# Query/key head norms of a fused decoder step: GpSimd's two multiplies go to VectorE, which reads the projections from PSUM

## The reference

```python
proj = rms_norm(x, norm_mix_g) @ w_in_ab      # 1024 -> 2*512 (GLU) + 512 q + 512 k + 512 v + 8 gates
q = rms_norm(q.reshape(*lead, H_B, HEAD_DIM), q_g)     # 8 heads of 64, one gain vector of 64
k = rms_norm(k.reshape(*lead, H_B, HEAD_DIM), k_g)     # k is also an output
glu = val * sigmoid(gate)                     # causal depthwise convolution of 31 taps, LayerNorm, swish
s = q @ k.T * HEAD_DIM ** -0.5 + F_q - F_k    # F: cumulative log forget gates; then softmax, @ v
```

## Time and profile before

| | us |
|---|---|
| median of 3 runs (lowest, highest) | 1314.85 (1314.0, 1315.89) |
| the profiled execution, its own time | 1313.07 |
| its span | 1311.3 |
| PE busy, share of the span | 1252.4, 96% |
| DVE busy | 625.4, 48% |
| ACT busy | 458.4, 35% |
| POOL busy | 165.7, 13% |
| the 30 steps of queries, keys and values | 83.2 to 204.9 |

### The profile page before, as it was taken

How to read it: one execution, slowest core, us unless ns; L and a number is a source line. 1 busy time by engine, 2 the same in 40 slices (tenths; PEclk the granted TensorE clock), 3 DMA queues, 4 the chain that set the end, 5 groups by cost and what they waited for, 6 DMA issues and landing times.

```text
span 1311.3 us, 22853 instructions
## 1 busy us (share of the span) xinstructions
PE 1252.4 (96%) x9658; PEld 1198.9 (91%) x9658; DVE 625.4 (48%) x860; ACT 458.4 (35%) x725; POOL 165.7 (13%) x181
## 2 busy tenths in 40 slices
PE   6987898889999999999999999989999999999998
PEld 5977885456999999999999999989999999999998
DVE  5597698745353343334244344664533342433431
ACT  5624435544343132132133334533421321321321
POOL 3036740100210000000000222042000000000000
PEclk9998998989999999999999999999999999999999
DMA  5321231133232322322222221213223223222211
GB/s 153 100 79 36 82 124 41 49 129 97 85 109 97 97 67 96 96 88 72 96 97 79 84 97 65 97 37 97 67 95 97 91 71 97 96 72 88 97 65 68
DMA packets 111755, 113.17 MB, mean 86 GB/s; under 512 B 6414, under 2 KB 105882, under 8 KB 111663
## 3 DMA queue, kind: packets, MB, share of 16 engines
q1 hardware_dynamic: 110111, 107.50, 25.4%
q0 software_dynamic: 1472, 4.44, 1.1%
q10 hardware_dynamic: 88, 0.02, 0.0%
HBM read 107.21 MB, written 5.16 MB: 86 GB/s over the span
## 4 chain that ended last, share of the span: by engine, by line
PE 82%; DVE 8%; POOL 4%; ACT 2%; issue 2%; DMA 1%; SPq 0%; ACTq 0%; POOLq 0%; DVEq 0%
PE ps L668 75%; DVE c_f L1521 3%; PE ps L859 2%; POOL nat_buf L571 2%; POOL nat_buf L578 1%; DMA w_raw<-in_w_in_ab 1%; PE ps L837 1%; PE ps L814 1%; DVE w_lo L1445 1%; PE ps L850 1%; DVE prob L1618 1%; POOL A_lo L643 1%; DVE a_f L1836 1%; ACT nat_sq L1189 1%; POOL nat_buf L576 0%
## 5 line engine op out<-in xcount | busy, mean ns | idle before, releaser
L668 PE MATMUL ps<-A_hi,w_hi 128*128 128x272 f32 x1408 | 293.2, 289 | 8.1 <-DVE xT L1471 4.0
L668 PE MATMUL ps<-A_lo,w_hi 128*128 128x272 f32 x1408 | 291.8, 289 | 0.0
L668 PE MATMUL ps<-A_hi,w_lo 128*128 128x272 f32 x1408 | 290.8, 288 | 0.0
L1110 ACT ACTIVATE w_hi<-w_raw 128x1024 fp32r<-128x1024 f32 x180 | 189.0, 1050 | 266.0 <-DVE xT L1733 249.2
L668 PE MATMUL ps<-B_hi,w_hi 128*128 128x272 f32 x1280 | 265.9, 289 | 0.0
L668 PE MATMUL ps<-B_lo,w_hi 128*128 128x272 f32 x1280 | 265.0, 288 | 0.0
L668 PE MATMUL ps<-B_hi,w_lo 128*128 128x272 f32 x1280 | 263.9, 288 | 0.0
L668 PEld LDWEIGHTS ps<-A_hi,w_hi 128*128 128x128 f32 x1408 | 221.7, 189 | 9.7 <-ACT xT L1140 4.4
L1445 DVE TENSOR_TENSOR w_lo<-w_raw,w_hi 128x1024 fp32r<-128x1024 f32 x180 | 220.3, 1224 | 4.7 <-ACT w_hi L1110 4.7
L668 PEld LDWEIGHTS ps<-A_hi,w_lo 128*128 128x128 f32 x1408 | 221.7, 189 | 0.0
L668 PEld LDWEIGHTS ps<-A_lo,w_hi 128*128 128x128 f32 x1408 | 220.4, 189 | 0.0
(11 more groups left out here) (273 smaller groups left out, 1057.0 us busy)
## 6 DMA issues: line engine op xcount, KB each, us to landing
w_raw<-in_w_ff_up SPq DMA_DIRECT2D x64, 512.0 KB, 4.4
w_raw<-in_w_ff_down SPq DMA_DIRECT2D x64, 512.0 KB, 4.3
w_raw<-in_w_in_ab SPq DMA_DIRECT2D x20, 512.0 KB, 4.7
w_raw<-in_w_in_c SPq DMA_DIRECT2D x16, 512.0 KB, 3.9
w_raw<-in_w_out_ab SPq DMA_DIRECT2D x8, 512.0 KB, 4.5
k_pg<-in_cache_k SPq DMA_DIRECT2D x16, 256.0 KB, 4.1
v_pg<-in_cache_v SPq DMA_DIRECT2D x16, 256.0 KB, 3.2
w_raw<-in_w_out_c SPq DMA_DIRECT2D x8, 512.0 KB, 4.0
```

Of the source, the lines that this page charges most:

```text
L668: mm = pe.matmul(ps[:, 2 * s + half, 0:HALF], wt[:, j % 4, k, :], mv[:, k, half * HALF:(half + 1) * HALF], start=(k == 0 and at_ == 0), st ...
L1110: act.activation(w_hi[:, j % 4], w_raw[:, b % 2, :, P * (j % 2):P * (j % 2) + P], ACT.Copy)\
```

## The change

POOL's two multiplies and ACT's copy `nat_raw` go away. DVE now does per step: the sums, then for the step before it the reciprocal, a multiply of the reciprocals by `r_nat` (128x4), a multiply of the PSUM bank by them into `nat_buf`, and for keys alone a multiply by the key gain. The query gain (times 1/8) is applied by ACT's copy of the transposed heads, as a scale per partition (`q_gain`, 66x1, with ones for the two forget rows). POOL copies the forget columns and stores keys. The square of step m no longer waits for POOL, but for the sums of step m - 2 (`nat_rs`). PE waits for DVE's product (`nat_evac`, `nat_ready`) and for POOL's columns (`cols_ok`). `nat_evac` is raised by DVE for steps 0 to 19, `v_evac` by ACT for the value steps. The convolution is dealt out anew: 19 in the GLU part (the last GLU step has 2 in place of 5), 3 in each query step, 2 in each key step, the value steps as before, and 19 in attention (where 16 were left before). `split_lo(11, 11)` moves from ahead of step 0 into step 1.

```diff
-CONV_GLU, CONV_QK, CONV_V = [6, 6, 5, 5], (2, 3), 4
-CONV_ATT = [1] * 18 + [0] * 14
+CONV_GLU, CONV_Q, CONV_K, CONV_V = [6, 6, 5, 2], (3, 3), (2, 2), 4
+CONV_ATT = [1] * 19 + [0] * 13
...
+            link(pool.memset(q_gain[:, :], 1.0))
+            pool.dma_start(q_gain[0:HD, :], i["q_norm_g"].rearrange("a d -> d a")).then_inc(q_gain_in, 16)
+            pool.dma_start(k_gain[:, :], i["k_norm_g"][0:1, :].broadcast_to([P, HD])).then_inc(bc_in, 16)
...
+            for m in range(4 * TT):
+                forget_columns(m)
+                if m - 1 >= 2 * TT:
+                    store_keys(m - 1)
...
-                pe.wait_ge(nat_ready, m + 1)
+                if m < 2 * TT:
+                    pe.wait_ge(nat_evac, m + 1)
+                else:
+                    pe.wait_ge(nat_ready, m + 1 - 2 * TT)
+                pe.wait_ge(cols_ok, m + 1)
...
                     if m >= 2:
-                        act.wait_ge(nat_ready, m - 1)
+                        act.wait_ge(nat_rs, m - 1)
                     act.activation(nat_sq[0:n, m % 2, :], src, ACT.Square, scale=r_nat[0:n, t:t + 1]).then_inc(nat_sq_done, 1)
-                    act.activation(nat_raw[0:n, m % 2, :], src, ACT.Copy, scale=r_nat[0:n, t:t + 1]).then_inc(nat_evac, 1)
...
-                               ACT.Copy).then_inc(aug_evac, 1)
+                               ACT.Copy, scale=q_gain[:, :] if m // TT < 2 else 1.0).then_inc(aug_evac, 1)
...
+            def scale_heads(m):
...
+                dve.wait_ge(nat_sqrt, m + 1)
+                link(dve.reciprocal(head, n_small[0:n, 2 + m % 2, :]))
+                link(dve.tensor_scalar(head, head, r_nat[0:n, t:t + 1], None, ALU.mult))
+                if m >= 3:
+                    dve.wait_ge(aug_done, m - 2)
+                    if m - 3 >= 2 * TT:
+                        dve.wait_ge(k_stored[m % 3], 16 * len([u for u in range(2 * TT, m - 2) if u % 3 == m % 3]))
+                dve.tensor_tensor(buf, ps[0:n, m % 4, 0:256].rearrange("p (h d) -> p h d", h=4),
+                                  head.rearrange("p (h a) -> p h a", a=1).broadcast_to([n, 4, HD]), ALU.mult)\
+                   .then_inc(nat_evac, 1)
+                if blk >= 2:
+                    dve.wait_ge(nat_evac, m + 1)
+                    dve.tensor_tensor(buf, buf, k_gain[0:n, :].rearrange("p (a d) -> p a d", a=1).broadcast_to([n, 4, HD]),
+                                      ALU.mult).then_inc(nat_ready, 1)
...
-            split_lo(11, 11)
...
                 if 1 <= m < 4 * TT + 1:
-                    head_factor(m - 1)
+                    scale_heads(m - 1)
+                if m == 1:
+                    split_lo(11, 11)
```

More of the change, by code:

```diff
@@ L159, in build @@
         conv_wT = sb("conv_wT", [P, CT, 32], F32)
-        qk_gain = sb("qk_gain", [P, 2, HD], F32)
+        k_gain = sb("k_gain", [P, HD], F32)
+        q_gain = sb("q_gain", [HD + 2, 1], F32)
         bf_c = sb("bf_c", [H, 1], F32)
@@ L404, in keys @@
                 if b == 0:
-                    sp.wait_ge(nat_ready, 4 * TT)
+                    sp.wait_ge(nat_ready, 2 * TT)
                 if b == 2:
@@ L558, in _, with forget_columns @@
                 pool.tensor_tensor(prod[c % 2][:, :, :, :], window, taps, ALU.mult).then_inc(prod_done, 1)
-            for m in range(4 * TT):
+            def forget_columns(m):
                 blk, t = m // TT, m % TT
                 n = NS if t == 0 else P
-                buf, head = nat_buf[0:n, m % 3], n_small[0:n, 4 + m % 2, :]
-                pool.wait_ge(head_ok, m + 1)
-                pool.wait_ge(nat_evac, m + 1)
+                if m == 0:
+                    pool.wait_ge(fc_ok, 1)
                 if m >= 3:
@@ L570, in _, with store_keys @@
                         pool.wait_ge(k_stored[m % 3], 16 * len([u for u in range(2 * TT, m - 2) if u % 3 == m % 3]))
[L571 to L587, removed]
+                pool.tensor_copy(nat_buf[0:n, m % 3, :, HD:HD + 2],
+                                 f_aug[0:n, blk // 2, H * t + 4 * (blk % 2):H * t + 4 * (blk % 2) + 4, :]).then_inc(cols_ok, 1)
+            def store_keys(m):
+                blk, t = m // TT, m % TT
+                n, h0 = (NS if t == 0 else P), 4 * (blk - 2)
+                pool.wait_ge(nat_ready, m + 1 - 2 * TT)
+                dst = (o["k_sample"][0].rearrange("b q h d -> (b q) h d")[:, h0:h0 + 4, :] if t == 0 else
+                       o["k_prompt"][0, 0, P * (t - 1):P * t, h0:h0 + 4, :])
+                pool.dma_start(dst, nat_buf[0:n, m % 3, :, 0:HD]).then_inc(k_stored[m % 3], 16)
+            for m in range(4 * TT):
+                forget_columns(m)
+                if m - 1 >= 2 * TT:
+                    store_keys(m - 1)
+            store_keys(4 * TT - 1)
+            pool.wait_ge(v_evac, 2 * TT)
             store(o["v_prompt"][0, 0].rearrange("(t p) h d -> p t (h d)", p=P), v_nat[:, 1:TT, :])
@@ L826, in _ @@
                     pe.wait_ge(lo_done, N_NAT + 2 * blk + 2)
-                if m >= 4:
+                if 4 <= m < 4 * TT + 4:
                     pe.wait_ge(nat_evac, m - 3)
+                if m >= 4 * TT + 4:
+                    pe.wait_ge(v_evac, m - 4 * TT - 3)
                 if m == 2:
@@ L1203, in aug_copy @@
                 dst, h0 = (qT if m // TT < 2 else kT), 4 * (m // TT % 2)
+                if m == 0:
+                    act.wait_ge(gain_ok, 1)
                 act.wait_ge(aug_done, m + 1)
@@ L1581, in sums @@
                                   AX_X, ALU.add).then_inc(nat_rs, 1)
-            def head_factor(m):
-                n = NS if m % TT == 0 else P
+            def scale_heads(m):
+                blk, t = m // TT, m % TT
+                n = NS if t == 0 else P
+                head, buf = n_small[0:n, 4 + m % 2, :], nat_buf[0:n, m % 3, :, 0:HD]
                 dve.wait_ge(nat_sqrt, m + 1)
-                if m >= 2:
-                    dve.wait_ge(nat_ready, m - 1)
-                dve.reciprocal(n_small[0:n, 4 + m % 2, :], n_small[0:n, 2 + m % 2, :]).then_inc(head_ok, 1)
-            split_lo(11, 11)
+                link(dve.reciprocal(head, n_small[0:n, 2 + m % 2, :]))
[11 more added lines that the diff above has]
+                                      ALU.mult).then_inc(nat_ready, 1)
             dve.wait_ge(glu_done, CT)
```

17 lines of the change are left out of this document (8 added, 9 removed).

## The result

The changed kernel takes 1298.52 us (median of 4 runs, 1297.32 to 1299.46) against 1314.42 (1310.26 to 1315.89), a ratio of 0.9884 with a 95% interval of 0.9859 to 0.9908. Its profiled execution took 1299.2 us, its span is 1297.5. Measured again on another chip, it took 1301.0 against 1313.14, a ratio of 0.991 (0.9894 to 0.9926). Forecast were 1301.6 and a gain of 13.2; the two measurements gave 15.9 and 12.1, the two profiled spans 13.8.

The account below looks back on a forecast made before the run. The prediction took the ring over ACT, DVE and POOL, 4.4 us a step against PE's 3.46, as the bound. Gain 14.4 less 1.2 in attention made 13.2: 1314.85 - 13.2 = 1301.6 us, range 1297.5 to 1308.

Parts of the forecast that it names:

- The ring: Query, key and value steps: ACT's square, DVE's reciprocal, POOL's two multiplies, next square; 4.4 us per step, gone after the change.
- PE's waits: Before the transposes in query steps: PE waits for DVE's products six times, 0.1 to 1.2 us each, 4.3 in all.
- no stretch below full clock: Sign to look for in the profile after: the granted clock stays full between 91 and 190 us.
- The rival of the clock: PE's query-step gaps keep the clock low; two or three half-clock steps cost 2.1 us each: 1304 to 1306; chance 0.10.
- DVE's list: DVE's work from 90.43 to attention's first maximum: 97.7 us, ending at 188.1 alone, 190.2 with 2.1 of waiting.
- that rival: Convolutions beside POOL's copies and stores keep 0.80 us, not 0.663: 1306 to 1311; chance 0.14, shared with a costlier norm.
- The norm: DVE, each query or key step: reciprocal 0.20, small multiply 0.20, product from PSUM 0.33, together 0.73 us.
- The two first convolutions: DVE, behind `glu_new` at the start of its list: counted at 0.663 us each, like all convolutions.
- PE's list: PE's own work from 91.59: 93.8 us, ending at 185.4 alone; 3.46 us per undisturbed step.
- What attention gives back: Three more convolutions at attention steps 16, 17 and 18 cost 1.2 us, between 0 and 2.0.
- The sum: Whole kernel: gain 14.4 less 1.2 given back in attention, net 13.2 us, for 1301.6 us.
- the stretch: From the GLU transposes to attention step 0's maximum; the maximum moves from 204.57 to 190.2, gaining 14.4 us.

Follow-up runs that it names:

- the first experiments: New convolution tables and `w_lo` place alone on the kernel before: 1313.73 us, ratio 0.9992; conversely, the changed kernel with the old ones: 1303.46 us, ratio 0.9901.
- the deep buffers: Kernel before, POOL's multiplies kept, four buffers instead of two for `nat_raw` and reciprocals, square waiting for sums of m - 2: 1308.83 us, ratio 0.9954.
- the run whose longest wait for a product was 0.8: Changed kernel with ACT's copy first and without the `r_nat` multiply, plus two last-GLU-step convolutions moved to attention: 1301.28 us, ratio 0.9905.
- after: The changed kernel itself, against the kernel before: 1298.52 us, ratio 0.9884; measured again on another chip, 1301.0 us, ratio 0.991.

## Why the prediction was right, step by step

**The ring and its end.** Right: both directions of the first experiments and the waits show it. I had seen only the ring over ACT. The second ring, through the reciprocal that stands behind the next sums on DVE, was in neither the prediction nor my expectation of the deep buffers. The change leaves that order as it was, but takes POOL's multiplies out of the ring. A turn is then some 4.9 us for two steps (matmuls 2.87, square 0.48, sums 0.33, norm 0.81, transposes 0.44; an estimate from rows of this section and of the chains), less than PE's own list. So the number did not suffer, and that was luck and not foresight.

**PE's waits, 4.3 foretold, 5.2 measured.** The size is right, the places are not. I had six waits of at most 1.2, all for DVE. The first is 2.53, which brought back 1.2 GHz for three us ("no stretch below full clock" failed, at a price of 14 matmuls at 0.21 in place of 0.12 from start to start, 1.3 us). The rival of the clock was right that it falls again, for a shorter time than it supposed; in the run whose longest wait for a product was 0.8 it did not fall. Three of 2.1 together are for ACT's copy, which I had costed at nothing. ACT's timeline after:

```profile
112.50 0.30 ACT L1206 ACTIVATE n_small<-n_small,eps 32x4 f32<-32x4 f32 x1 [2.78 <-DVE n_small L1591]
112.70 0.66 ACT L1215 ACTIVATE qT<-ps,q_gain 66x512 f32<-66x512 f32 x1
```

The copy stands behind the root, the root waits for DVE's sums, and PE waited 1.01 us for the copy at 113.51.

**DVE's list, 99.8 foretold (with 2.1 of waits), 101.3 measured** (90.20 to 191.51). DVE's timeline after, beside the earlier trace rows:

```profile
90.20 3.31 DVE L1532 SCALAR_TENSOR_TENSOR c_f<-glu_p,conv_wT,c_f 128x512 f32<-128x512 f32 x2
93.42 0.40 DVE L1591 TENSOR_REDUCE n_small<-nat_sq 32x4 f32<-32x256 f32 x1
93.75 2.06 DVE L1532 SCALAR_TENSOR_TENSOR c_f<-glu_p,conv_wT,c_f 128x512 f32<-128x512 f32 x3
...
104.46 0.41 DVE L1591 TENSOR_REDUCE n_small<-nat_sq 128x4 f32<-128x256 f32 x1
104.79 0.16 DVE L1600 RECIPROCAL n_small<-n_small 128x4 f32<-128x4 f32 x1
104.99 0.23 DVE L1601 TENSOR_SCALAR n_small<-n_small,r_nat 128x4 f32<-128x4 f32 x1
105.25 0.42 DVE L1606 TENSOR_TENSOR nat_buf<-ps,n_small 128x256 f32<-128x256 f32 x1
105.60 2.06 DVE L1532 SCALAR_TENSOR_TENSOR c_f<-glu_p,conv_wT,c_f 128x512 f32<-128x512 f32 x3
...
138.10 0.16 DVE L1600 RECIPROCAL n_small<-n_small 128x4 f32<-128x4 f32 x1
...
139.01 0.43 DVE L1611 TENSOR_TENSOR nat_buf<-nat_buf,k_gain 128x256 f32<-128x256 f32 x1
139.36 1.41 DVE L1532 SCALAR_TENSOR_TENSOR c_f<-glu_p,conv_wT,c_f 128x512 f32<-128x512 f32 x2
...
175.60 15.98 DVE L1532 SCALAR_TENSOR_TENSOR c_f<-glu_p,conv_wT,c_f 128x512 f32<-128x512 f32 x24
191.51 0.28 DVE L1635 TENSOR_REDUCE soft<-ps 128x1 f32<-128x128 f32 x1
```

- The convolution, (191.51 - 175.60) / 24 = 0.663: right, beside POOL's copies too (2.06 for three at 105.60, with a copy from 106.43), so that rival falls.
- Sums 0.33 for 0.34; the product 105.60 - 105.25 = 0.35 for 0.33. The rule of the Trainium skill (VectorE: DVE Perf Modes, The TRN2 errata), 0.39 by estimate, is further off than the row that I took; the busy time of the product was 0.42.
- The norm, 105.60 - 104.79 = 0.81 for 0.73: the term of the sum that was sized too low, by about 1.5 us over 20 (0.08 for each of 16, 0.05 for the four of the sampled tokens). The small multiply took 0.26 to its follower where I had put 0.20, the price of the reciprocal. A key's norm with its gain took 139.36 - 138.10 = 1.26, 0.45 more than a query's, as foretold.
- The two first convolutions took 3.31 where two alone take 1.40: 1.9 us, the largest miss. The row was there in the earlier trace rows: five convolutions at 90.43 took 5.28 and not 3.4, beside POOL's product for the sampled tokens. I had looked at the row for the gap only, and not for POOL beside it.
- Against that, DVE's waits for squares were 1.2 and not 2.1, and `sum_taps` took 110.08 - 108.72 = 1.36, not 1.63.

**PE's list.** 3.29 us per step in place of 3.46: in the step that I had measured, PE's weight load still waited 0.2 us for POOL. PE and DVE came in 1 us apart (PE's last matmul of values at 190.32, DVE's maximum at 191.51), where 0.5 was foretold.

**What attention gives back,** 1.2 foretold, is 0.2 to 0.5. The prediction took the two convolutions ahead of the division as lost in full. But in these four steps after, PE waited for the division once, 0.3 us, and was busy 7.41 of the 7.92 us; in the whole of attention it waited 10 times for it, 10.9 us in sum, as before (11 times, 11.1).

**The sum.** 14.4 foretold for the stretch, 12.9 measured; 1.2 given back, 0.2 to 0.5 measured: 13.2 and about 12.5 net. The misses in DVE's list were of both signs (1.9 and 1.5 too low, 0.9 of waits and 0.5 of `sum_taps` too high), which helped. The first measurement of 15.9 has 3.4 us more than 12.5, the second, 12.1, has 0.4 less. Between the two first profiles the 13.8 us are 0.2 ahead of the stretch, 12.9 in it, 2.2 in attention, and 1.5 lost in the rest; what is beside the 12.9 moves by as much between two profiles of one kernel, so a hit within 2 us of the whole time says little.

## What to carry over

Write down every ring in which an engine's step feeds itself, the order of instructions in each list included: opening one ring by buffers gave 2.7 us of the stretch, and opening a second one, made by the order of two lines, gave 5.7 more. When work moves to the engine that will set the end, count each small dependent instruction at its start-to-start time, and look at what the neighbour engine runs beside the first few. The version with the best whole time here keeps the change, puts ACT's copy ahead of its root, and takes one four-column multiply per step off DVE: 1295.88 us against 1314.07, with a stretch 3.6 us shorter than the change alone. Its ratio of 0.9863 (0.9847 to 0.988) overlaps the interval of after's first measurement and not that of its second.

## What the runs showed of the hardware

- DVE beside POOL, by the size of POOL's work. POOL's timeline after, then DVE's and POOL's of the run with no convolution in the last GLU step:

```profile
90.36 2.60 POOL L560 TENSOR_TENSOR prod<-glu_s,conv_wT 128x992 f32<-128x992 f32 x1 [12.50 <-DVE glu_new L1574]
```

```profile
93.22 3.22 DVE L1533 SCALAR_TENSOR_TENSOR c_f<-glu_p,conv_wT,c_f 128x512 f32<-128x512 f32 x3
```

```profile
92.43 2.14 POOL L561 TENSOR_TENSOR prod<-glu_s,conv_wT 128x992 f32<-128x992 f32 x1 [12.50 <-DVE glu_new L1577]
```

  Of the 2.60 us side by side DVE lost 1.9 in the first, and of the 1.35 (93.22 to 94.57) it lost 1.2 in the second. So most of the shared time is lost to DVE, and taking the two convolutions away made the next three pay part of it. With 256-column multiplies on POOL in each step the mean loss was 63 ns per convolution between 104 and 168 us, those that ran alone included.
- ACT's copy of 66x512 from PSUM took 0.667 us with a scale per partition and 0.576 with a constant one, 0.09 more.
- One kernel's attention came out at 73.6 and 77.4 us with all work the same, and what differed was the granted clock. The rest behind attention took 1029.2 to 1032.4 us in the runs here, with the same code. Differences of a few us in the whole time need the length of the changed stretch beside them.
